# A two-block model on one core: 24 modulation units of the second block move to other stages

## What is computed

```python
# second block (cut)
for l in range(DEPTH):
    mod = silu(c) @ w_ada[l] + b_ada[l]                  # 1024 x 6144 weights a layer
    sh1, sc1, g1, sh2, sc2, g2 = split(mod, 6)
    h = rmsnorm(x, norm_mix_g[l]) * (1 + sc1) + sh1
    x = x + g1 * mixer(h)                                # conv and attention, then w_out
    h = rmsnorm(x, norm_ffn_g[l]) * (1 + sc2) + sh2
    x = x + g2 * (swiglu(h) if l == 0 else moe_swiglu(h))
```

## Time and profile before

| | |
|---|---|
| median of 3 runs | 2348.11 us (2348.02 to 2352.99) |
| the profiled execution | 2352.04 us |
| its span in the profile | 2350.2 us |
| mean granted TensorE clock | 0.974 of full speed |
| busy: PE, DVE, ACT | 2225.8, 1794.5, 1323.7 us |
| first block, layers 0 and 1 | to about 380 us and 690 us |
| first mixer of the second block | 690 to 869 us, attention loop about 765 to 831 us |
| feed-forward part | 869 to about 1062 us |
| second mixer, then experts | to about 1260 us, to the end |

### The profile page before, as it was taken

The page is one execution under the profiler, slowest core; times in us unless marked ns, Lnnn a source line. Parts: engine busy times, 40 slices in busy tenths (PEclk is TensorE's granted clock), DMA queues, the critical chain, the costliest instruction groups (busy, mean ns, idle before and its releaser), DMA issues.

```text
span 2350.2 us, 34455 instructions
## 1 busy us (share of the span) xinstructions
PE 2225.8 (95%) x13371; PEld 1915.1 (81%) x13371; DVE 1794.5 (76%) x2236; ACT 1323.7 (56%) x1219; POOL 31.3 (1%) x61
## 2 busy tenths in 40 slices
PE   6999999999989889998886999999999999999998
PEld 4899998999988379998656887878787887878786
DVE  4978767777667757775864888878787888888886
ACT  3555546555553154434223767676767667676774
POOL 3000000000000000000000000000000000000000
PEclk9999999999999999999887999999999999999999
DMA  9778755666545428775341899999999999999994
GB/s 290 222 228 247 229 168 161 198 202 210 180 161 185 161 91 280 263 261 177 135 147 53 312 331 348 334 345 336 336 344 325 353 332 345 332 346 333 338 340 179
DMA packets 357043, 597.06 MB, mean 254 GB/s; under 512 B 10408, under 2 KB 201400, under 8 KB 356936
## 3 DMA queue, kind: packets, MB, share of 16 engines
q1 hardware_dynamic: 353632, 589.02, 73.0%
q0 software_dynamic: 2912, 6.42, 1.2%
q10 hardware_dynamic: 392, 0.13, 0.0%
HBM read 594.46 MB, written 4.22 MB: 255 GB/s over the span
## 4 chain that ended last, share of the span: by engine, by line
PE 82%; DVE 9%; ACT 4%; issue 3%; SPq 1%; DMA 1%; DVEq 0%; ACTq 0%
PE ps L1371 8%; PE ps L1373 8%; PE ps L1372 8%; PE ps L961 7%; PE ps L962 7%; PE ps L963 7%; PE ps L1399 4%; PE ps L1400 4%; PE ps L1398 4%; PE ps L986 3%; PE ps L987 3%; PE ps L988 3%; DVE wlo L1457 2%; ACT whi L652 2%; PE ps L1245 2%
## 5 line engine op out<-in xcount | busy, mean ns | idle before, releaser
L1457 DVE TENSOR_TENSOR wlo<-raw,whi 128x2048 fp32r<-128x2048 f32 x487 | 1112.4, 2289 | 353.0 <-ACT whi L652 333.9
L652 ACT CAST whi<-raw 128x2048 fp32r<-128x2048 f32 x487 | 928.2, 1907 | 424.5 <-PE ps L1373 139.2
L961 PE MATMUL ps<-hhi,whi 128*128 128x256 f32 x1424 | 411.7, 289 | 10.8 <-DVE zpad L1822 8.7
L962 PE MATMUL ps<-hlo,whi 128*128 128x256 f32 x1424 | 404.9, 284 | 0.0
L963 PE MATMUL ps<-hhi,wlo 128*128 128x256 f32 x1424 | 404.6, 284 | 0.0
L1371 PE MATMUL ps<-whi,xghi 128*128 128x512 f32 x896 | 365.5, 408 | 9.9 <-DVE wlo L1457 8.4
L1373 PE MATMUL ps<-wlo,xghi 128*128 128x512 f32 x896 | 354.0, 395 | 0.0
L1372 PE MATMUL ps<-whi,xglo 128*128 128x512 f32 x896 | 353.9, 395 | 0.0
L961 PEld LDWEIGHTS ps<-hhi,whi 128*128 128x128 f32 x1424 | 275.0, 193 | 16.8 <-DVE zpad L1822 9.5
L962 PEld LDWEIGHTS ps<-hlo,whi 128*128 128x128 f32 x1424 | 275.3, 193 | 0.2
L963 PEld LDWEIGHTS ps<-hhi,wlo 128*128 128x128 f32 x1424 | 275.0, 193 | 0.0
(11 more groups left out here) (378 smaller groups left out, 3166.6 us busy)
## 6 DMA issues: line engine op xcount, KB each, us to landing
raw<-in_moe_w_gate_dram SPq DMA_DIRECT2D x114, 1024.0 KB, 5.2
raw<-in_moe_w_up_dram SPq DMA_DIRECT2D x112, 1024.0 KB, 5.2
raw<-in_moe_w_down_dram SPq DMA_DIRECT2D x112, 1024.0 KB, 4.9
raw<-in_w_in_dram SPq DMA_DIRECT2D x92, 1024.0 KB, 5.3
raw<-in_w_ada_dram SPq DMA_DIRECT2D x69, 1024.0 KB, 7.9
raw<-in_w_out_dram SPq DMA_DIRECT2D x24, 1024.0 KB, 4.9
raw<-in_ffn_w_gate_dram SPq DMA_DIRECT2D x11, 1024.0 KB, 5.7
raw<-in_ffn_w_up_dram SPq DMA_DIRECT2D x11, 1024.0 KB, 7.8
```

The source lines that it names most:

```text
L652: nc.scalar.copy(whi[:, u.hl, :], raw[:, u.raw, :]).then_inc(hi_ready, 1)
L961: mm(ps2[u.bank][:, j], whi[:, u.hl, w], hhi[:, k], start=k == 0, stop=False)
L962: mm(ps2[u.bank][:, j], whi[:, u.hl, w], hlo[:, k], start=False, stop=False)
L1457: V.tensor_tensor(wlo[:, u.hl, :], raw[:, u.raw, :], whi[:, u.hl, :].bitcast(F32), ALU.subtract).then_inc(raw_free, 1)
```

## The change

The units are spread anew; their number stays 72. Layer 1 of the first block gets 9 a pair (18 in all) instead of 6 (12), with the pattern of layer 0. The first mixer gets none instead of 10, and with them go its `cpad`, `arow` and the turning. The feed-forward part gets 24 instead of 16, at three of four places instead of every second. The second mixer gets 4 instead of 8. Each unit's values still go to `mod` before they are used.

```diff
-ADA_START, ADA_TURN, ADA_MIX, ADA_FF = 8, (9, 6), (10, 8), 16
+ADA_START, ADA_TURN, ADA_MIX, ADA_FF = 8, (9, 9), (0, 4), 24
...
-def ada_beside(l, j):
-
-    if l == 0:
-        return j // 2 if j >= 0 and j % 2 == 0 else None
-    return j // 3 if j >= 0 and j % 3 == 1 else None
+def ada_beside(j):
+
+    return j // 2 if j >= 0 and j % 2 == 0 else None
+
+
+def ada_beside_ff(j):
+
+    return j - j // 4 if j >= 0 and j % 4 != 3 and j - j // 4 < ADA_FF else None
...
-ADA_AT_FF = [(Ada(A_FF + i, A_FF), 1, 1, i) for i in range(ADA_FF)]
+ADA_AT_FF = [(Ada(A_FF + i, A_FF), 1) + ((0, 20 + i) if i < 4 else (1, i - 4)) for i in range(ADA_FF)]
...
@@ SP, the feed-forward part (the down units alike)
-                if j % 2 == 0 and j // 2 < ADA_FF:
-                    ada_load(*ADA_AT_FF[j // 2])
+                if ada_beside_ff(j) is not None:
+                    ada_load(*ADA_AT_FF[ada_beside_ff(j)])
...
@@ ACT, the mixer
-                act.wait_ge(ada_done, (A_MIX0, A_MIX1)[l] + ADA_MIX[l])
-                nc.scalar.copy(arow[0:ADA_MIX[l]], ps[0][0:ADA_MIX[l], 0:S]).then_inc(arow_ready, 1)
+                if l:
+                    act.wait_ge(ada_done, ADA_UNITS)
+                    nc.scalar.copy(arow[0:ADA_MIX[l]], ps[0][0:ADA_MIX[l], 0:S]).then_inc(arow_ready, 1)
...
@@ PE, the attention loop
-                    extra = rows - NH2
-                    ada_rows(n + min(n, extra))
+                    if n < rows:
+                        ada_rows(n)
                     pe.wait_ge(p2_ready, n0 + n + 1)
...
                     last.then_inc(pT_done, 1)
-                    if n < extra:
-                        ada_rows(2 * n + 1)
                     pe.wait_ge(pT_ready, n0 + n + 1)
...
@@ PE, after the first unit of the mixer's output projection
-                        pe.wait_ge(arow_ready, l + 1)
-                        for i in range(2):
-                            last = nc.tensor.transpose(...)
-                        last.then_inc(arow_turned, 1)
+                        if l:
+                            (the same)
...
@@ PE, the feed-forward part
-                if j % 2 == 0 and 1 <= j // 2 <= ADA_FF:
-                    ada(ADA_AT_FF[j // 2 - 1][0], ps[7])
+                if ada_beside_ff(j - 1) is not None:
+                    ada(ADA_AT_FF[ada_beside_ff(j - 1)][0], ps[7])
...
@@ DVE, the mixer's start
-                step(V.memset(cpad[:], 0.0))
-                V.tensor_copy(cpad[:, :, max(ADA_MIX) - 1:max(ADA_MIX)], cact[:, 1].unsqueeze(2)).then_inc(cpad_ready, 1)
+                if l:
+                    (the same)
...
@@ DVE, the feed-forward part (the down units alike)
-                if j % 2 == 0 and j // 2 < ADA_FF:
-                    ada(*ADA_AT_FF[j // 2])
+                if ada_beside_ff(j) is not None:
+                    ada(*ADA_AT_FF[ada_beside_ff(j)])
...
             dve.wait_ge(ada_done, A_MIX1)
-            take_mod(ps[7], 0, ADA_FF, *ADA_AT_FF[0][1:]).then_inc(mod_taken, 1)
-            dve.wait_ge(mod_taken, 6)
+            take_mod(ps[7], 0, 4, *ADA_AT_FF[0][1:])
+            take_mod(ps[7], 8, ADA_FF - 4, *ADA_AT_FF[4][1:]).then_inc(mod_taken, 1)
+            dve.wait_ge(mod_taken, 5)
```

More of the change, by code:

```diff
@@ L191, in ada_l1 @@
     first = A_L1 + pair * ADA_TURN[1]
-    return [(Ada(first + i, first), 1, 0, pair * 6 + (2 + i)) for i in range(ADA_TURN[1])]
-def ada_beside(l, j):
-    if l == 0:
-        return j // 2 if j >= 0 and j % 2 == 0 else None
-    return j // 3 if j >= 0 and j % 3 == 1 else None
+    return [(Ada(first + i, first), 1, 0, pair * ADA_TURN[1] + (2 + i)) for i in range(ADA_TURN[1])]
+def ada_beside(j):
+    return j // 2 if j >= 0 and j % 2 == 0 else None
+def ada_beside_ff(j):
+    return j - j // 4 if j >= 0 and j % 4 != 3 and j - j // 4 < ADA_FF else None
 ADA_AT_START = [(Ada(i, 0), 0, 0, i // 2 + ADA_START // 2 * (i % 2)) for i in range(ADA_START)]
@@ L505, in _ @@
                     at = j % (2 * HEAD_UNITS)
-                    if at and ada_beside(l, at - 1) is not None:
-                        ada_load(*(ada_l0, ada_l1)[l](pair)[ada_beside(l, at - 1)])
+                    if at and ada_beside(at - 1) is not None:
+                        ada_load(*(ada_l0, ada_l1)[l](pair)[ada_beside(at - 1)])
                 for j in range(OUT1_UNITS):
@@ L1286, in mixer @@
                     if j == 0:
-                        pe.wait_ge(arow_ready, l + 1)
-                        for i in range(2):
-                            last = nc.tensor.transpose(ps[0][:, S + rows * i:S + rows * i + rows], arow[0:rows, P * i:P * i + P],
-                                                       ident[0:rows, 0:rows])
-                        last.then_inc(arow_turned, 1)
+                        if l:
+                            pe.wait_ge(arow_ready, 1)
+                            for i in range(2):
+                                last = nc.tensor.transpose(ps[0][:, S + rows * i:S + rows * i + rows], arow[0:rows, P * i:P * i + P],
+                                                           ident[0:rows, 0:rows])
+                            last.then_inc(arow_turned, 1)
                         pe.wait_ge(zsq_ready, l + 1)
@@ L1871, in mixer @@
                     low(Unit(first + MIX_UNITS + LOOK + j))
[L1872 to L1880, removed]
+                if l:
+                    dve.wait_ge(arow_turned, 1)
+                    rows, of = ADA_MIX[l], P2_BADA + 2 * (ADA2 - ADA_MIX[l])
+                    to = 3 * KD * (3 * l + 1) + of - P2_BADA
+                    for i in range(2):
+                        last = V.tensor_tensor(mod[:, to:to + 2 * rows].rearrange("p (u j) -> p j u", j=2)[:, i],
+                                               ps[0][:, S + rows * i:S + rows * i + rows],
+                                               par2[:, l, of:of + 2 * rows].rearrange("p (u j) -> p j u", j=2)[:, i],
+                                               ALU.add)
+                    last.then_inc(mod_taken, 1)
                 dve.wait_ge(zstd_ready, l + 1)
@@ L1918, in _ @@
                     low(Unit(S_FF + FF_UNITS + j + LOOK))
-                if j % 2 == 0 and (FF_UNITS + j) // 2 < ADA_FF:
-                    ada(*ADA_AT_FF[(FF_UNITS + j) // 2])
+                if ada_beside_ff(FF_UNITS + j) is not None:
+                    ada(*ADA_AT_FF[ada_beside_ff(FF_UNITS + j)])
                 if j == 0:
```

22 lines of the change are left out of this document (11 added, 11 removed).

## The result

The changed kernel takes **2366.93 us** (median of 7 runs, 2362.17 to 2368.53), the kernel before beside it 2348.85 (7 runs): ratio 1.0066, 95% interval 1.0052 to 1.0081. It is slower by 12 to 19 us. The forecast was 2362, range 2351 to 2369.

The account below looks back on a forecast made before the run. PE, with 82% of the chain of waits, was taken to bound the kernel. The terms 2.9 + 2.2 + 3.7 + 1.7 - 0.3 + 3.2 - 0.1 + 0.9 = +14.2 us, from 2348.1, gave 2362, range 2351 to 2369.

Parts of the forecast that it names:

- Forecast 7.6: Layer 1: six units on PE +2.2 us, two waits for `sT` +3.7, one half-clock drop +1.7.
- One drop in two: Layer 1: one of the two `sT` waits is followed by half clock over 3.4 us, +1.7 us (bounds 0 and 3.4).
- Forecast +2.8: First mixer: -0.3 us at its start, +3.2 for loop and tail at half clock, -0.1 behind the projection's first unit.
- The tail of 2.3: First mixer, last value product to output projection: 2.44 us becomes up to 4.9 at half clock, taken as +2.3.
- the rival: Attention loops: the clock holds at 2.4 GHz in the emptied heads, so not slower, 2347 us; chance 0.12.
- The value product of head 4 stays at 1195.72: Second mixer: the first heads, which keep their units, take as long as before, so head 4's value product does not move.
- the way out: Second mixer, behind the last value product: 2.3 us more to the projection at half clock, 0.7 for the slow start.
- I take 0: Feed-forward part, SP's queue: modulation loads that wait and hold up the next weight load cost 0 us.
- one of the signs named for being wrong: Feed-forward part: PE waiting on DVE beside the units would show the forecast wrong.
- the third rival: Feed-forward part: DVE becomes the bound, PE loses 1 us in each of 5.5 groups, +5.5 us, 2368; chance 0.15.
- DVE's sum: Feed-forward part: four weight units with three modulation units take DVE 23.9 us against PE's 24.3, so DVE just keeps up.

Follow-up runs that it names:

- e1_layer1: The kernel before with only layer 1's modulation units changed to nine a pair, the six additional units computed twice: 2360.49 us, ratio 1.0049.
- e4_order: The changed kernel with DVE's fourth modulation step of a head put behind `sT` instead of before `arg`, in both layers of the first block: 2357.28 us, ratio 1.0031.
- e2_loads: The changed kernel with each modulation load beside the feed-forward part issued two weight loads later: 2363.39 us, ratio 1.0063.
- e10_last_head: The changed kernel with later modulation loads, the modulation step behind `sT` and idle matmuls in the attention loops, except eight in each mixer's last head: 2334.38 us.
- e9_repaired: The changed kernel with later modulation loads, the modulation step behind `sT`, and idle matmuls in heads without a unit and in `pT` waits: 2338.47 us, ratio 0.9955.

## Why the prediction was right, and where it was not

The sign was right, and the median of 2366.93 lies in the range, 4.6 above the forecast. That the sum of +14.2 meets the 14.1 between the profiled executions is luck. Against the forecast the stages are off by +0.8 (layer 1), -1.0 (first mixer), +2.6 (feed-forward part), -5.3 (second mixer) and +2.8 (the rest), and these cancel to -0.1. The median grew by 18.1: of the profiled executions that of before stood 3.2 above the median of its seven runs and that of after 0.8 below, and I had expected both to stand 3.9 above.

- **Layer 1: right.** Forecast 7.6, measured 8.4, and 7.8 alone in e1_layer1. Two waits of 1.84, one drop of the clock for 3.4 us and six units on PE, all as put. e4_order took all but the last away. "One drop in two" for these waits was a guess from two cases: before has one behind its two waits, the changed kernel one behind its four, since the one of layer 0 did not come again (the 5.3 us behind that wait were at 0.68 before and are at 1.00 after).
- **First mixer: right in mechanism, 1.0 too high.** Forecast +2.8, measured +1.8. The loop went to half clock and stayed there. A head is 8.97 us, not 8.79: DVE's and ACT's part is 5.81, as taken from before, but PE's is 3.15 and not 2.98. The tail of 2.3 came as forecast (4.70 - 2.44). What was missed lies in front of the loop. The first value product starts 99.0 us after the stage's start, where its `pT` was ready at 101.1 before (775.4, the anchor of the prediction): 2.1 earlier, of which the forecast had 0.3 for `cpad`. It is not the first head's lost units, as PE's first scores start 2.1 us earlier already (772.39 - 683.8 = 88.6 after, 764.96 - 674.3 = 90.7 before). Less half clock goes with it: the 20 us from 690 on were at 0.81 before, the 20 us at the same distance from the stage's start at 0.91 after. e1_layer1, which keeps all units of this mixer, is 1.0 below before in it as well, so part of the 2.1 has nothing to do with the change.
- **The rule of the skill.** The Trainium skill (TensorE: Matmul & The Clock Gate, "Loop structure matters more than you think") says that VectorE's copy out of PSUM doesn't break PE's warmth, for a loop in which the next iteration's matmuls follow immediately. Here they don't follow: PE waits for just such a copy, `pT` (1.15 us), and for DVE's probabilities before it (3.80 us), and the clock is at 0.50 from 803 to 830 us. So the rival had carried the rule over to a loop for which the page doesn't state it.
- **Second mixer: wrong.** Forecast +0.9, measured -4.4. The heads without units went as put: from the fourth head's value product to the last, 28.6 us against 30.3, -1.7 for -2.1. Two steps failed. The first is "The value product of head 4 stays at 1195.72": the two drops of the clock in the first heads were taken as fixed, and of both only a short one came, 3.6 us less. They don't belong to the loop alone, and with two drops of 2.1 us these heads should have had a range of 0 to -4.2 of their own. The second is the way out: forecast 2.3 to the projection and 0.7 behind it, together +3.0, measured +0.6. The way to the projection takes 4.18 us (1234.46 - 1230.28) against 2.43 in the kernel before, where it starts at 1220.92 (1220.92 - 1218.49), +1.7; from there to the stage's end it is 1.1 less, as a drop that before has too was shorter (8 us around it at 0.79 instead of 0.57).
- **Feed-forward part: mis-sized.** Forecast 2.9, measured 5.5. The step that failed is SP's, "I take 0": a load that waits for `ada_done` at three of four places holds the weight load behind it back, and that lands late (8.7 and 8.6 us after its issue, 5.8 and 6.7 in e2_loads). PE waiting on DVE here was one of the signs named for being wrong, and it came twice. It was the third rival's symptom, half its size, with another cause. DVE's sum (23.9 in 24.3) was good: in e2_loads it kept up.
- **Not forecast:** 2.8 us in stages that the change doesn't touch. Of these, -1.8 go with the missing drop in layer 0. The 1.7 behind the second mixer go with a clock of 0.72 against 0.75 in its first 54 us; the 2.9 at the start are open, and other profiles have 0.4 to 3.2 there.

## What to carry to other kernels

Work that fills PE's pauses in a loop with a latency chain can hold the granted clock up (here 1.00 with it and 0.50 without it in the same 27 us, though in the second mixer it did not always). Before such work is moved away, price the loop at both clock levels, and if it goes, try idle matmuls in the pauses themselves. Whatever is put at more places of an engine's order must be followed through the queue that loads it: a load that waits on a semaphore delays every load issued behind it. And place side work on DVE behind the result for which PE waits next, not in front of it.

## What was not expected of the hardware

- Idle matmuls paid for themselves. Eleven useless matmuls in a head without a unit, three in the others, made the two mixers 13 us shorter than the changed kernel's. Eight alone, which left a pause of 1.5 us at `pT`, gave a clock that swung from head to head in the one profile taken (9.65 and 7.56 us); with three more in that pause it was 1.00 and every head 7.56.
- The same pause does or doesn't cost a drop from one kernel to the next: behind the `sT` waits at 478.78 there was one and at 607.59 none, behind `y2lo` one in e10_last_head and none in e9_repaired, and in the second mixer's first heads two before and a short one after. Each is worth about 1.5 to 2.1 us, the short one 0.6 (8.18 - 7.56). I could not forecast which falls where, and two kernels that differ by less than a few such drops are hard to rank by one profile.
